# Adding expert outputs to HBM rows by an accumulating indirect transfer instead of storing and gathering them

## The reference

```
x  = x + mod[2] * token_mixer(modulate(rms_norm(x, g_mix), ...))          # x1 in the kernel
h  = modulate(rms_norm(x, g_ffn), mod[3], mod[4])
x  = x + mod[5] * hier_moe(h)            # top-1 of 4 groups, top-2 of its 4 experts
out = rms_norm(x, final_norm_g)

hier_moe: y = sum over 16 experts e of gates[:, e] * ((silu(h @ wg[e]) * (h @ wu[e])) @ wd[e])
```

## Time and profile before

| | us |
|---|---|
| median of 3 runs (1093.82 to 1095.35) | 1094.55 |
| the profiled execution's span | 1087.6 |
| PE busy | 898.1 (83%) |
| DVE busy | 750.3 (69%) |
| ACT busy | 415.2 (38%) |
| POOL busy | 374.9 (34%) |
| expert loop, from the first ysc (571.4) to the last (ends 1032.3) | 461 |
| from the last ysc to the end of the span | 55 |

### The profile page before, as it was taken

How to read it: one execution, slowest core, us unless ns; L and a number is a source line. 1 busy time by engine, 2 the same in 40 slices (tenths; PEclk the granted TensorE clock), 3 DMA queues, 4 the chain that set the end, 5 groups by cost and what they waited for, 6 DMA issues and landing times.

```text
span 1087.6 us, 12479 instructions
## 1 busy us (share of the span) xinstructions
PE 898.1 (83%) x3689; PEld 630.0 (58%) x3690; DVE 750.3 (69%) x890; ACT 415.2 (38%) x520; POOL 374.9 (34%) x181
## 2 busy tenths in 40 slices
PE   6789999569898989992279998999999899988900
PEld 2354444224345468882268886888888677776700
DVE  2235999997993353446885768567655988888658
ACT  1333535125445221114142445335514555555312
POOL 1000806600000000002254637266241777766671
PEclk9999999789899999995589998999999888889955
DMA  8884413306214513316556748475462888887494
GB/s 319 290 329 155 139 36 96 96 1 207 82 41 163 224 58 116 116 78 233 192 188 238 270 162 305 189 270 212 162 244 77 305 319 304 324 319 281 153 362 198
DMA packets 108564, 213.48 MB, mean 196 GB/s; under 512 B 11006, under 2 KB 47996, under 8 KB 108540
## 3 DMA queue, kind: packets, MB, share of 16 engines
q1 hardware_dynamic: 97996, 174.37, 44.2%
q0 software_dynamic: 5904, 21.50, 5.5%
q10 hardware_dynamic: 4640, 17.30, 3.9%
HBM read 180.12 MB, written 33.03 MB: 196 GB/s over the span
## 4 chain that ended last, share of the span: by engine, by line
PE 47%; DVE 34%; issue 8%; DMA 4%; DVEq 4%; ACT 3%; SPq 0%; POOL 0%; ACTq 0%; POOLq 0%
DVE WP L1519 7%; PE bank L696 7%; DVE macc L1327 5%; PE bank L903 3%; PE bank L881 3%; PE bank L883 3%; PE bank L882 3%; PE bank L904 3%; PE bank L905 3%; PE bank L809 3%; PE bank L810 3%; PE bank L811 3%; DVE rkt L1533 2%; PE bank L678 2%; DVE fb L1643 2%
## 5 line engine op out<-in xcount | busy, mean ns | idle before, releaser
L616 POOL TENSOR_TENSOR WP<-raw,WP 128x1024 fp32r<-128x1024 f32 x64 | 186.7, 2947 | 0.7 <-ACT WP L1133 0.5
L696 PE MATMUL bank<-hT,wring 128*128 128x512 f32 x384 | 168.5, 597 | 2.6 <-ACT hT L961 1.9
L1519 DVE TENSOR_TENSOR WP<-raw,WP 128x2048 fp32r<-128x2048 f32 x62 | 156.8, 2569 | 11.3 <-ACT WP L1129 8.2
L1129 ACT ACTIVATE WP<-raw 128x2048 fp32r<-128x2048 f32 x64 | 119.5, 1917 | 89.8 <-issue 76.6
L881 PE MATMUL bank<-WP,xp 128*128 128x512 f32 x368 | 143.9, 391 | 1.5 <-DVE xp L1556 1.5
L883 PE MATMUL bank<-WP,xp 128*128 128x512 f32 x368 | 143.8, 391 | 0.0
L882 PE MATMUL bank<-WP,xp 128*128 128x512 f32 x368 | 143.6, 390 | 0.0
L696 PEld LDWEIGHTS bank<-hT,wring 128*128 128x128 f32 x384 | 73.4, 192 | 93.5 <-issue 90.1
L628 POOL TENSOR_TENSOR WP<-raw,WP 128x2048 fp32r<-128x2048 f32 x2 | 9.0, 4536 | 300.4 <-ACT WP L1129 300.4
L612 POOL TENSOR_TENSOR held<-held 128x1 f32<-128x1 f32 x24 | 36.2, 1509 | 218.1 <-DVE idg L1548 210.5
L1327 DVE SCALAR_TENSOR_TENSOR macc<-mring,silu_c,macc 128x256 f32<-128x256 f32 x112 | 88.7, 792 | 4.0
(11 more groups left out here) (278 smaller groups left out, 1478.3 us busy)
## 6 DMA issues: line engine op xcount, KB each, us to landing
raw<-in_expert_w_gate SPq DMA_DIRECT2D x64, 512.0 KB, 3.9
raw<-in_expert_w_up SPq DMA_DIRECT2D x64, 512.0 KB, 6.3
raw<-in_expert_w_down SPq DMA_DIRECT2D x64, 512.0 KB, 7.2
mring<-in_mod_w SPq DMA_DIRECT2D x20, 1024.0 KB, 5.0
expert_rows<-ysc ACTq DMA_DIRECT2D x23, 512.0 KB, 7.3
expert_rows<-g SPq DMA_DIRECT2D x16, 512.0 KB, 11.4
wring<-in_w_in SPq DMA_DIRECT2D x12, 512.0 KB, 5.9
mslot<-in_mod_w SPq DMA_DIRECT2D x4, 1024.0 KB, 14.7
```

Of the source, the lines that this page charges most:

```text
L616: pool.tensor_tensor(WP[:, j, 1, 2 * D:], raw[:, j, 2 * D:], WP[:, j, 0, 2 * D:].bitcast(F32), ALU.subtract).then_inc(s_lod[j], 1)
L696: mm = pe.matmul(o_, wring[:, n % 3, k, :], src, start=k == 0, stop=k == KD - 1)
L1129: A_(WP[:, j, 0, 0:2 * D], raw[:, j, 0:2 * D], ACT.Copy).then_inc(s_hgu, 1)
L1519: tt(WP[:, j, 1, 0:2 * D], raw[:, j, 0:2 * D], WP[:, j, 0, 0:2 * D].bitcast(F32), ALU.subtract).then_inc(s_logu[j], 1)
```

## The change

ysc is no longer stored by slot and gathered by token. POOL adds each of its 128 rows to the row of x1_d of its token, by an indirect DMA with addition at the destination. x1_d gets 128 rows more; a row of a slot that holds no token is added to row 1024 + p there. The row numbers are the token ids where the gate is over zero, and 1024 + p (the constant dump) elsewhere; DVE makes them in slot_gates, in fp32, and slot_rows turns one column into int32 just before the scaling. POOL's scatter of a slot stands after its four subtractions; it waits for ysc and the row numbers, runs a one-element instruction on held, issues the transfer, and waits until it has landed. POOL thus never has two of them under way. DVE's scaling waits for held instead of the store's semaphore. y_d, its zeroing, pos, the final gathers and the sums go; after s_end SP loads x1 back in eight tiles, and ACT and DVE normalise each.

```diff
-    x1_d = nc.dram_tensor("mixed_rows", [SEQ, D], F32).ap()
-    y_d = nc.dram_tensor("expert_rows", [MAXT, P, D], F32).ap()
+    x1_d = nc.dram_tensor("mixed_rows", [SEQ + P, D], F32).ap()
...
-            sp.wait_ge(s_zero, 1)
-            for r in range(NE, MAXT):
-                sp.dma_start(y_d[r], g5[:]).then_inc(s_zero_d, 16)
...
-            sp.dma_start(fx[:, 0:4], x1v[:, 0:4]).then_inc(s_fl[0], 16)
             sp.dma_start(gfin[:], final_g.partition_broadcast(P)).then_inc(s_gf, 16)
             sp.wait_ge(s_end, 1)
-            sp.dma_start(fx[:, 4:8], x1v[:, 4:8]).then_inc(s_fl[1], 16)
+            for t in range(NT):
+                sp.dma_start(fx[:, t], x1v[:, t]).then_inc(s_fl[t], 16)
...
                 if not isinstance(q, int):
-                    hold(q - 2)
+                    hold(2 * (q - 2))
...
+            def scatter(s, p2):
+                pool.wait_ge(s_ye, 2 * s + 4)
+                pool.wait_ge(s_row, s + 1)
+                pool.wait_ge(s_held, 2 * s + 2)
+                pool.tensor_tensor(held[:], held[:], held[:], ALU.mult).then_inc(s_held, 1)
+                pool.indirect_dma_start(out=x1_d, out_offset=bass.IndirectOffsetOnAxis(ap=rowi[:, p2], axis=0),
+                                        in_=ysc[:, p2, :], in_offset=None, compute_op=ALU.add).then_inc(s_sc, 16)
+                pool.wait_ge(s_sc, 16 * s + 16)
...
                         with pool.If(L > 0):
                             for j in range(KE):
                                 split_down(E1, j)
-
-            Wl = pool.value_load(tab[0:1, 3, 1:2], min_val=NE, max_val=MAXT)
-            Wf = pool.value_load(tab[0:1, 3, 2:3], min_val=NE, max_val=MAXT)
-            pool.wait_ge(s_ys[0], 8 * Wl + 16)
-            pool.wait_ge(s_ys[1], 8 * Wf + 16)
+                        scatter(s, par)
+
             pool.wait_ge(s_xg, 16 * W + 32)
-            hold(W)
+            hold(2 * W)
             pool.memset(stat[:, 63:64], 0.0).then_inc(s_end, 1)
-            y_rows = y_d.rearrange("s p d -> (s p) d")
-            for t in range(NT):
-                for a, buf in enumerate((fa, fb)):
-                    pool.indirect_dma_start(out=buf[t][:], out_offset=None, in_=y_rows,
-                                            in_offset=bass.IndirectOffsetOnAxis(ap=pos[:, a, t:t + 1], axis=0))\
-                        .then_inc(s_fg[t], 16)
-            for t in POOL_SUMS:
-                pool.wait_ge(s_fg[t], 32)
-                pool.tensor_tensor(fa[t][:], fa[t][:], fb[t][:], ALU.add).then_inc(s_fps, 1)
...
-                        act.wait_ge(s_ye, 2 * s + 4)
-                        act.dma_start(y_d[bass.ds(s, 1)].rearrange("a p d -> (a p) d"),
-                                      ysc[:, par, :]).then_inc(s_ys[par], 16)
...
             def slot_gates(q, p2):
 
-                dve.tensor_reduce(gcol[:, p2], idf[:, 2:5], AX.X, ALU.add).then_inc(s_pch, 1)
+                col = rowf[:, q:q + 1] if isinstance(q, int) else rowf[:, bass.ds(q, 1)]
+                plink(q, dve.tensor_reduce(gcol[:, p2], idf[:, 2:5], AX.X, ALU.add), 2)
+                plink(q, ts(occ[:, 0:1], gcol[:, p2], 0.0, None, ALU.is_gt), 3)
+                plink(q, stt(out=occ[:, 1:2], in0=idf[:, 0:1], scalar=idf[:, 1:2], in1=K("dump"), op0=ALU.add,
+                             op1=ALU.subtract), 4)
+                stt(out=col, in0=occ[:, 1:2], scalar=occ[:, 0:1], in1=K("dump"), op0=ALU.mult,
+                    op1=ALU.add).then_inc(s_pch, 1)
+
+            def slot_rows(q, p2):
+
+                dve.wait_ge(s_pch, NLINK * q + 5)
+                dve.tensor_copy(rowi[:, p2], rowf[:, bass.ds(q, 1)]).then_inc(s_row, 1)
...
-            link(tt(Gp, RK[:].rearrange("p e t -> p t e"), sq128.unsqueeze(1).to_broadcast([P, NT, NE]), ALU.add))
...
-            link(dve.tensor_copy(pos[:, 0, :], p1))
-            link(dve.tensor_copy(pos[:, 1, :], p2))
...
                         dve.wait_ge(s_dd, 4 * s + 4)
-                        dve.wait_ge(s_ys[par], 16 * it + 16)
+                        dve.wait_ge(s_held, 2 * s + 1)
+                        slot_rows(s, par)
...
             for t in range(NT):
-                final_sum(t)
-                if t >= 1:
-                    final_row(t - 1)
-            final_row(NT - 1)
+                final_row(t)
```

More of the change, by code:

```diff
@@ L150, in build @@
         held = keep("held", [P, 1])
-        pos = keep("pos", [P, 2, NT], I32)
         PHASE = cursor[0]
@@ L231, in build @@
         gcol = at("gcol", [P, 2, 1], F32, o); o += 32
+        occ = at("occ", [P, 2], F32, o); o += 32
+        rowf = at("rowf", [P, TAB], F32, o); o += 160
+        rowi = at("rowi", [P, 2, 1], I32, o); o += 32
         tab = at("tab", [1, 4, TAB], I32, o); o += 640
@@ L274, in build @@
         s_sph, s_spl, s_scr = sem("split_hi"), sem("split_lo"), sem("ffn_scale_ready")
-        s_zero = sem("zero_row")
-        s_zero_d = sem("sums_zeroed")
         s_pvp = sem("params_transposed")
@@ L354, in build @@
         s_ye = sem("y_scaled")
-        s_ys = [sem(f"y_stored{n}") for n in range(2)]
+        s_row = sem("slot_rows_ready")
+        s_sc = sem("y_added")
         s_held = sem("pool_held")
@@ L364, in build @@
         s_pch = sem("prepare_chain")
-        s_fps = sem("expert_rows_added")
-        s_fg = [sem(f"expert_rows_in{n}") for n in range(NT)]
         s_gb3 = sem("shift_scale_bias_in")
         s_gff = sem("ffn_gain_in")
-        s_fl = [sem(f"x1_back{n}") for n in range(2)]
-        s_fx1 = sem("final_sum")
+        s_fl = [sem(f"x1_back{n}") for n in range(NT)]
         s_fs = sem("final_square")
@@ L398, in build @@
         mod_fill = lambda n: n // 4 + 1 if n < 2 * MCH else 2 * MCH // 4 + (n - 2 * MCH) // 2 + 1
-        POOL_SUMS = (3, 4, 5, 6)
         XPARTS = (range(0, 2), range(2, 6), range(6, 10))
@@ L471, in _ @@
                 if n == 5:
-                    sp.wait_ge(s_zero_d, 16 * (MAXT - NE))
                     sp.dma_start(g5[:], everywhere(mod_b[0:1, 5 * D:6 * D])).then_inc(s_gb5, 16)
@@ L494, in _ @@
                 sp.dma_start(xr[t][:], xv[:, t]).then_inc(s_xr[t], 16)
-            x1v = x1_d.rearrange("(t p) d -> p t d", p=P)
+            x1v = x1_d[0:SEQ].rearrange("(t p) d -> p t d", p=P)
             xnv = xn_d.rearrange("(t p) d -> p t d", p=P)
@@ L551, in _ @@
         def _(pool):
-            pool.memset(g5[:], 0.0).then_inc(s_zero, 1)
             pool.memset(held[:], 0.0).then_inc(s_held, 1)
@@ L1138, in hi_rows @@
                    ACT.Copy).then_inc(s_xgh, 1)
-            for n in range(2):
-                act.sem_inc(s_ys[n], 16)
             for j in range(KE):
@@ L1175, in _ @@
                                 hi_down(E1, j)
-                        act.wait_ge(s_ye, 2 * s + 4)
-                        act.dma_start(y_d[bass.ds(s, 1)].rearrange("a p d -> (a p) d"),
-                                      ysc[:, par, :]).then_inc(s_ys[par], 16)
             for t in range(NT):
-                act.wait_ge(s_fx1, t + 1)
+                act.wait_ge(s_fl[t], 16)
                 if t >= 2:
@@ L1520, in lo_gate_up @@
                    ALU.subtract).then_inc(s_logu[j], 1)
-            NLINK = 2
+            NLINK = 5
             def plink(q, ins, k):
@@ L1572, in _ @@
             prepare_slots(2, E2, T2)
-            Gp, sq128, p2, p1 = m16(G), every(1500, NE), every(1520, NT), every(1530, NT)
-            link(ts(sq128, sq_all, float(P), None, ALU.mult))
-            link(tt(Gp, RK[:].rearrange("p e t -> p t e"), sq128.unsqueeze(1).to_broadcast([P, NT, NE]), ALU.add))
-            link(tt(m16(R_["big"]), m16(M2), Gp, ALU.mult))
-            link(dve.tensor_reduce(p2, m16(R_["big"]), AX.X, ALU.add))
-            link(tt(Gp, m16(M1), Gp, ALU.mult))
-            link(dve.tensor_reduce(p1, Gp, AX.X, ALU.add))
-            link(tt(p1, p1, p2, ALU.subtract))
-            link(dve.tensor_copy(pos[:, 0, :], p1))
-            link(dve.tensor_copy(pos[:, 1, :], p2))
             W = dve.value_load(tab[0:1, 3, 0:1], min_val=NE, max_val=MAXT)
@@ L1626, in _ @@
             dve.wait_ge(s_gf, 16)
-            def final_sum(t):
-                if t in POOL_SUMS:
-                    dve.wait_ge(s_fps, POOL_SUMS.index(t) + 1)
-                else:
-                    dve.wait_ge(s_fg[t], 32)
-                    link(tt(fa[t][:], fa[t][:], fb[t][:], ALU.add))
-                if t % 4 == 0:
-                    dve.wait_ge(s_fl[t // 4], 16)
-                tt(fx[:, t], fx[:, t], fa[t][:], ALU.add).then_inc(s_fx1, 1)
             def final_row(t):
```

## The result

The changed kernel takes 1127.13 us, the median of four runs (1125.89 to 1129.76); beside them the kernel before took 1094.18. The ratio is 1.031 (95% interval 1.029 to 1.034): 3.1% slower. The forecast of 1100 had the sign right and the size wrong, and 1127 lies above its range. The profiled execution's span went from 1087.6 to 1123.7 us.

The account below looks back on a forecast made before the run. It took DVE's waits for POOL's subtractions, the two taking turns, as the bound. Terms -25.5 - 3.7 + 8.8 + 14.5 + 12 = +6.1 us gave a 1093.7 span, predicted 1100.7, rounded 1100; range 1071 to 1121.

Parts of the forecast that it names:

- On-time slots: Expert-loop slots whose gather is in time: both scalar_tensor_tensor wait for POOL's subtractions, oh ending at 17.5 us, not 14.8.
- s-s: Eight loop slots with an expert change after them and after the next: 0.65 us each if on time, 8.8 in all.
- s-n: Seven slots with an expert change after them but none after the next: sg up to 2.75 us later, 14.5 together.
- plain slots: Loop slots after which the expert stays: new instructions hidden in DVE's waits; 12 us from a halved clock in four.
- The clock: PE's 2.97 us wait for sg would halve the granted clock in four slots: 12 us, bounds 0 and 14.
- Copy and ts: DVE's new one-element instructions per slot: would not wait for POOL's subtractions; 6 us more in sum if they did.
- gcol's side: Assumption that one-element DVE instructions, like the reduction gcol at 0.16 us, run amid POOL's subtractions without waiting.
- the price of a late gather: In the loop, a gather late behind the scatter's landing: sg comes 1.4 us later, since the engines keep taking turns.
- Rival 3: Accumulating transfer lands later than 9 us after issue, so POOL's cycle bounds s-s slots: 1121 us at 12; chance 13%.
- The end: From the last y scaled to the kernel's end: 29.7 us instead of 55.3, gain 25.5 (22 to 27).
- The positions: Instructions L1575 to L1583 before the loop removed: first sg 4.6 us earlier, 0.9 lost again, gain 3.7.
- The zeroing: Sixteen 512 KB stores from 54.36 us removed: cost and gain 0, at most 1 us gained.

Follow-up runs that it names:

- e2_defer: Changed kernel with POOL waiting for a scatter's landing only before the next scatter, and for the last behind the loop: 1091.34 us.
- e4_dve_only: Kernel before the change plus only DVE's new instructions, results unused, POOL scattering nothing: 1120.48 us.
- e3_both: Changed kernel with both scalar_tensor_tensor written as tensor_scalar and the landing awaited only before the next scatter: 1066.07 us.
- e1_ts: Changed kernel with its two scalar_tensor_tensor written as tensor_scalar with two scalar columns: 1090.00 us.
- e5_late_before: Kernel before the change with the one-element instruction on held run three times ahead of each gather, making POOL late: 1157.62 us.
- e7_gap: Changed kernel with a 0.1 us memset behind each of POOL's four subtractions in the loop: 1113.19 us.
- e9_gap_defer: Changed kernel with the landing awaited only before the next scatter and a memset behind each of POOL's four subtractions: 1075.41 us.

## Why the prediction was wrong, point by point

**On-time slots: right in the mechanism, a quarter too dear.** With the late slots taken at their on-time length (three s-s at 5.9 less, two s-n at 5.9 and 5.6 less, 29.2 in all) the changed kernel's loop would sum to +2.1 in s-s, +12.8 in s-n, and +10.4 in plain slots, 25.4 together. The forecast's terms were 8 x 0.65 = 5.2, 14.5 and 12, 31.7 together.

The clock fell in the four plain slots for which it was forecast (3, 8, 10 and 12 take 20.4 to 21.6 us, and 18.9 before), and in slot 6 (20.3), behind the late slot 5. Slots 8 and 3, then slot 1 (bounds, us, busy PE, PEld, DVE, ACT, POOL, clock, DMA, GB/s):

```profile
740.10:746.90 6.80, 6.80 (x19) 5.40 (x19) 1.66 (x5) 0.66 (x2) 0.38 (x2) 0.56 0.37 67
624.10:630.90 6.80, 6.80 (x26) 5.45 (x25) 2.37 (x6) 1.74 (x4) 0.01 (x1) 0.56 0.50 82
...
584.33:591.13 6.80, 6.80 (x32) 5.61 (x33) 2.33 (x7) 0.77 (x2) 0.50 (x2) 1.00 0.39 75
```

PE is busy through all three. In slots 8 and 3 the granted clock is 0.56, most of each stretch at the lower level of 1.2 GHz, and PE has waited 2.56 us for sg before (0.22 in the earlier trace rows). But in slot 1 it has waited 2.57 us, and the clock stays at 1.00 and the slot at 18.9 us; in e2_defer the same wait before slot 1 is followed by 0.57, and the slot takes 21.4. So the length of this one wait does not settle what the clock does, and no run shows what else does. (The window of half the clock in the earlier trace rows follows PE's wait in slot 16, which was 2.04 us, not the 1.91 of slot 17 shown above it.) e4_dve_only measured the terms by themselves: 24.1 us in the slots, against 31.7 forecast.

**Copy and ts: right.** They took gcol's side in all 23 slots (0.15 us). The rule of the Trainium skill ("Vector Engine (DVE) Microarchitecture Reference", section 5.1) said the same, and the trace agrees.

**The failed step: the price of a late gather.** The prediction said that POOL might be late in s-s slots, and gave 9 to 13 us needed against 9.7 there; ahead of slot 15's gather it was 13.8 (1.35 hold, 3.48 issue, 7.0 to the landing, and 1.9 of POOL's own register loads and branches behind the wait, which I had not counted). The point from which it counts was right too: the end of the third split. But I priced a late start at 1.4 us, by letting the engines go on taking turns. It costs 6, five times, because they don't: 8.8 forecast for s-s, and 19.8 measured, and 11.5 more in two s-n slots, for which no lateness was forecast at all. The late slots' share is 29.2 us measured against 3.6 forecast (8 x 0.45), 25.6 too little; the on-time terms were 6.3 too high, from the last ids to the last ysc 2.1 came on top (6.4 us against 4.3), and 0.3 went from the first sg to the first ids. That makes the 21 us by which the loop was missed. e2_defer shows the step by itself: with the gathers on time the slots sum to 28.7 us less. Rival 3, whose end of 1121 was nearest (by its own count of one microsecond in all eight slots, 3 x 8, it is 1124), reached it by a landing 12 us behind the issue; in the slots that made the next one late it was 6.9 to 7.3 behind it, and 4.3 in slot 20.

**The end: 5 us too good.** The chain of waits after the last scatter, start and duration:

```profile
1089.70 5.94 DMA mixed_rows<-ysc,rowi
1095.70 0.12 issue
...
1099.33 0.05 POOLq L638
...
1099.89 3.27 DMA fx<-mixed_rows
1103.18 1.15 ACT fj L1167 x2
```

The landing took 5.94 us (5.5 forecast), the first tile 3.3 (3), the rows come 1.81 apart. So the tiles arrived fast enough, which the forecast's row had not shown: 8.9 us for 2 MB are 2.2 for a tile. What the forecast didn't have are 3.9 us between landing and end of the loop: POOL's loop has 32 passes, and the nine without a slot are still to be gone through, behind the wait. In e2_defer, where the wait stands behind the loop, the last hold comes 7.2 us after the last ysc ends instead of 10.8.

**The positions: 2.5 us too low.** Without them the split does not wait for POOL's fourth subtraction, as the step had it, but goes ahead of it, and 2.56 us of register loads that stood bare behind pos (up to 557.53 in the trace of before) lie under waits:

```profile
551.96 3.38 DVE L1519 TENSOR_TENSOR oh<-cst,rkt 128x1024 bf16<-128x1024 f32 x1
555.27 4.49 DVE L1502 TENSOR_TENSOR WP<-raw,WP 128x2048 fp32r<-128x2048 f32 x1
559.93 0.69 DVE L1579 SCALAR_TENSOR_TENSOR sg<-sg,bank 128x512 f32<-128x512 f32 x1 [0.17 <-ACT sg L1147]
```

**The zeroing: 0, as forecast**, as far as a profile can tell: kernels with it (535.0 and 534.8, and before with 531.5) and without it (534.7 to 538.9) reach their first ids at times that scatter by 3 to 4 us, which would hide a microsecond or two. The zeroing was not tested by itself.

The sum closes: 6.1 forecast, +21.1 (loop), +5.0 (end), -2.5 (positions), +6.4 (the stretch before the first gather, of which no part is shown to be the change) give 36.1 us, the difference of the spans.

## What to carry to other kernels

A wait put into an engine's queue is priced not only by how long it lasts, but by where the work behind it then falls against the other engine's: here five late starts cost 29 us, and moving one wait to just before the next transfer got them back. Before a small instruction is placed beside POOL's work, look whether it reads two SBUF tensors; the same arithmetic with the second operand as a scalar column cost next to nothing (the slots of e3_both sum to 0.6 us more than before's), where the first form cost 26 us in 23 slots. And when a wait moves to the last pass of a loop, count what the engine still has to run through after it.

## What the runs showed of the hardware that I had not expected

- **Taking turns holds only from a contended start.** Where POOL's first subtraction began inside DVE's third split and had to wait for it, the engines alternate, one instruction each, for the rest of the slot (1.3 us before the split's end, in every on-time slot of every kernel). Where it started 0.9 to 1.2 us after the split's end, the four run through in 9.4 us (2.36 each), and a DVE instruction that asks 0.6 to 2.9 us after the start gets its turn only at the end: 8.9 us (after), 6.9 (e1_ts), 7.7 (e5_late_before, 15 of 15). The Trainium skill ("SBUF — State Buffer", Who interferes with whom) says that the one that starts first holds the shared ports for its whole instruction, and the other blocks until then. By this alone the wait would be 2.4 us at most; the traces show it over three and four instructions. Why the start decides is open: a 0.1 us memset between the subtractions did not change it, and a longer gap was not tried.
- **A gap of 0.1 us can let in a second small instruction** behind one that has just had its turn (0.22 us instead of 2.45, in 8 of 10 on-time slots of e7_gap and 6 of 15 of e9_gap_defer), worth 14 us in e7_gap.
- **One-element instructions with one SBUF tensor never waited**, also with two scalar columns (0.27 us in all 23 slots of e3_both), while rkt, with 8 elements, did (0.82 at the median there).
- **The accumulating scatter of 512 KB** landed 5.9 us after its issue began where nothing else ran, 6.3 at the median, 10.4 to 10.8 where its issue fell beside a split and weights were loading (7.8 beside a split without them); the one without the addition 3.4, 4.2 and 8.1.
